# Three stage borders of a hybrid decoder layer: own buffers for the first output-projection weights, first MLP weights split ahead of the norm, operand differences ahead of weight sums

## What is computed

```python
h = modulate(rms_norm(x), shift1, scale1)
y = hybrid_mixer(h, ...)            # ends in concatenate([o_gla, o_hgrn]) @ w_out
x = x + gate1 * y
h = modulate(rms_norm(x), shift2, scale2)
y = square(relu(h @ w_mlp1)) @ w_mlp2
x = x + gate2 * y
return rms_norm(x, final_norm_g)
```

## Time and profile before

| | |
|---|---|
| median of 3 runs | 1274.1 us (1270.65 to 1276.03) |
| the profiled execution | 1274.15 us, its span 1272.4 us |
| TensorE matmul busy | 1174.3 us (92%) |
| VectorE, ScalarE, GpSimd busy | 845.0, 581.1, 484.4 us |
| mean granted TensorE clock | 0.961 |

### The profile page before, as it was taken

One profiled execution on the slowest core, in us unless ns is written; L12 is line 12 of the kernel. 1 busy time (PEld: TensorE's weight loads), 2 busy tenths in 40 slices (PEclk: granted clock), 3 DMA queues, 4 the chain that ended last, 5 costly groups with the idle time before them and its releaser, 6 DMA issues.

```text
span 1272.4 us, 15360 instructions
## 1 busy us (share of the span) xinstructions
PE 1174.3 (92%) x5519; PEld 959.0 (75%) x5519; DVE 845.0 (66%) x970; ACT 581.1 (46%) x865; POOL 484.4 (38%) x286
## 2 busy tenths in 40 slices
PE   4288999989999999699799999999989999999987
PEld 3166778778888887588587888888868888888875
DVE  7978377645454445545498777656796596886965
ACT  4324345444646536324455554554562343424314
POOL 3742101102112112322454434432465575675740
PEclk8589989989999999799999999999989999999999
DMA  8644234101111010434135535345622745547203
GB/s 297 189 155 153 83 117 150 34 17 36 48 33 45 21 50 18 133 97 135 67 99 165 182 133 163 118 158 174 209 72 59 255 128 173 205 125 276 73 1 132
DMA packets 148667, 151.95 MB, mean 119 GB/s; under 512 B 6180, under 2 KB 117880, under 8 KB 145912
## 3 DMA queue, kind: packets, MB, share of 16 engines
q1 hardware_dynamic: 148600, 151.07, 37.0%
HBM read 116.97 MB, written 34.08 MB: 119 GB/s over the span
## 4 chain that ended last, share of the span: by engine, by line
PE 74%; DVE 14%; issue 5%; ACT 4%; POOL 1%; DMA 1%; DVEq 0%; SPq 0%; ACTq 0%; POOLq 0%
PE unit_bank L1221 24%; PE unit_bank L1496 7%; PE unit_bank L1498 7%; PE unit_bank L1497 7%; PE small_bank L1496 7%; PE small_bank L1498 7%; PE small_bank L1497 7%; DVE ada_acc L1549 3%; PE small_bank L1221 2%; PE small_bank L1255 2%; PE small_bank L1344 2%; DVE state L1689 1%; PE small_bank L1336 1%; DVE a_lo L1535 1%; DVE op_lo L1821 1%
## 5 line engine op out<-in xcount | busy, mean ns | idle before, releaser
L1221 PE MATMUL unit_bank<-a_hi,w_hi 128*128 128x512 f32 x592 | 241.9, 409 | 29.9 <-DVE w_lo L1742 12.4
L756 POOL TENSOR_TENSOR wr_lo<-quarter,wr_hi 128x512 fp32r<-128x512 f32 x122 | 197.2, 1630 | 181.1 <-ACT wr_hi L1073 181.1
L1221 PE MATMUL unit_bank<-a_hi,w_lo 128*128 128x512 f32 x592 | 234.7, 397 | 0.0
L1221 PE MATMUL unit_bank<-a_lo,w_hi 128*128 128x512 f32 x592 | 234.5, 396 | 0.0
L693 POOL TENSOR_TENSOR w_lo<-raw,w_hi 128x1024 fp32r<-128x1024 f32 x29 | 75.3, 2595 | 353.2 <-ACT w_hi L795 353.2
L1496 PE MATMUL unit_bank<-op_hi,wr_hi 128*128 128x512 f32 x452 | 179.4, 397 | 18.2 <-POOL wr_lo L756 6.8
L1498 PE MATMUL unit_bank<-op_hi,wr_lo 128*128 128x512 f32 x452 | 178.3, 394 | 0.0
L1497 PE MATMUL unit_bank<-op_lo,wr_hi 128*128 128x512 f32 x452 | 178.0, 394 | 0.0
L1496 PE MATMUL small_bank<-op_hi,wr_hi 128*128 128x512 f32 x452 | 176.6, 391 | 0.0
L1497 PE MATMUL small_bank<-op_lo,wr_hi 128*128 128x512 f32 x452 | 176.0, 389 | 0.0
L1498 PE MATMUL small_bank<-op_hi,wr_lo 128*128 128x512 f32 x452 | 175.9, 389 | 0.0
(11 more groups left out here) (224 smaller groups left out, 1823.8 us busy)
## 6 DMA issues: line engine op xcount, KB each, us to landing
quarter<-in_w_mlp_dram SPq DMA_DIRECT2D x128, 256.0 KB, 4.5
hidden_scratch<-hid SPq DMA_DIRECT2D x98, 256.0 KB, 2.9
ada_slot<-in_w_ada_dram SPq DMA_DIRECT2D x48, 512.0 KB, 4.7
op_full<-hidden_scratch SPq DMA_DIRECT2D x21, 1024.0 KB, 4.8
raw<-in_w_in_dram SPq DMA_DIRECT2D x29, 512.0 KB, 3.7
raw<-in_w_out_dram SPq DMA_DIRECT2D x16, 512.0 KB, 3.9
x_stage<-in_x_dram SPq DMA_DIRECT2D x8, 512.0 KB, 4.1
x_scratch<-xT SPq DMA_DIRECT2D x2, 2048.0 KB, 8.0
```

Source lines behind the costliest of these rows:

```text
L756: pool.tensor_tensor(wr_lo[slot][:, :, :], split_source(n), wr_hi[slot][:, :, :].bitcast(F32), ALU.subtract).then_inc(wr_lo_pool, 1)
L1221: return pe.matmul(out_ap, left, right, start=start, stop=stop)
```

## The change

At border 1, four new buffers `first_w_hi0/1` and `first_w_lo0/1` lie over `k_end`, `k_rel`, `q_rel` and `q_cum`, and hold the weights of output units 0 and 1. ScalarE rounds them after the first quarter of the last gate, VectorE makes the remainders of 0 there, of 1 and 2 behind `low_mixed(0)`, of 3 ahead of `low_mixed(1)`. Units 2 and 3 use the old buffers.

At border 2, `high_weights` 0 and 1 move into the v loop (v = 13), 2 to 6 ahead of `inverse_rms(1)`. The inverse root is a Sqrt on ScalarE and a `reciprocal` on VectorE that writes into the PSUM bank the sum came from; `scale_half` reads that bank. Products 6 and 14, which reuse those banks, wait for the scaling.

At border 3, the P5 parts move one step ahead (DOWN - 2), with both P5 differences; the P6 differences (`second_sum`) stand in step DOWN - 1, and the weight sums and the weight rounding for product 120 move to the end of that step.

```diff
-    parts = {DOWN - 8: (P1,), DOWN - 1: (P5, P3), DOWN: (P2, P7), DOWN + 1: (P6,), DOWN + 2: (P4,)}.get(n, ())
+    parts = {DOWN - 8: (P1,), DOWN - 2: (P5,), DOWN - 1: (P3,), DOWN: (P2, P7), DOWN + 1: (P6,), DOWN + 2: (P4,)}.get(n, ())
...
+        first_w_hi = [at(f"first_w_hi{v}", kb, [P, KT, P], F32R) for v, kb in enumerate((128, 136))]
+        first_w_lo = [at(f"first_w_lo{v}", kb, [P, KT, P], F32R) for v, kb in enumerate((132, 140))]
...
                 if v < 2:
-                    act.wait_ge(unit_filled[1], U_OUT + v - 1)
+                    act.wait_ge(filled["sc" if v else "k"], before("sc" if v else "k", 7))
+                elif v < 4:
+                    act.wait_ge(unit_filled[1], U_OUT + v - 3)
...
+                        if idx == 0:
+                            high_out(0)
+                            high_out(1)
...
                         if half == 1:
-                            high_out(j)
+                            high_out(2 + j)
...
-                act.activation(tok(t0, half), SB[2 + half][:, :], ACT.Ln, bias=eps, scale=1.0 / D
+                act.activation(tok(t0, half), SB[2 + half][:, :], ACT.Sqrt, bias=eps, scale=1.0 / D
                                ).then_inc(read["stat"], 1)
-                act.wait_ge(read["stat"], half + 1)
-                act.activation(tok(t0, half), tok(t0, half), ACT.Exp, scale=-0.5).then_inc(rms_ready, 1)
...
+                if v == 13:
+                    for n in range(2):
+                        high_weights(n)
...
-            for n in range(2):
+            for n in range(2, RING):
                 high_weights(n)
             inverse_rms(1)
-            for n in range(2, RING):
-                high_weights(n)
...
-                if n + RING < PRODUCTS:
+                if n + RING < PRODUCTS and n != DOWN - 1:
                     high_weights(n + RING)
...
                 first_down(n)
+                if n == DOWN - 1:
+                    high_weights(n + RING)
...
                         if idx == 2:
                             low_mixed(0)
+                            low_out(1)
+                            low_out(2)
                         read_out(4 + idx)
                         gate(u0 + 2 + j, 6 + idx, 6 + j, half, idx % 2)
+                        if idx == 0:
+                            low_out(0)
+                    low_out(3)
                     low_mixed(1)
...
+            def inverse_rms(half):
+
+                dve.wait_ge(read["stat"], half + 1)
+                dve.reciprocal(SB[2 + half][:, :], tok(t0, half)).then_inc(rms_ready, 1)
+                dve.wait_ge(rms_ready, 3 + half)
...
-                if n >= 2:
+                if n >= 2 and n != DOWN - 1:
                     hidden_sums(n - 2)
+                if n == DOWN - 2:
+                    hidden_sums(n - 1)
+                if n == DOWN - 1:
+                    for x in range(2):
+                        second_sum(g, x)
                 first_down(n)
+                if n == DOWN - 1:
+                    weight_sums(n + RING)
```

More of the change, by code:

```diff
@@ L436, in out_done, with out_weights @@
             return U_OUT + v % KT + 1
+        def out_weights(v):
+            return (first_w_hi[v], first_w_lo[v]) if v < 2 else (w_hi[(U_OUT + v) % 2], w_lo[(U_OUT + v) % 2])
         def wait_low(e, n):
@@ L1038, in high_half @@
                                ).then_inc(h_high, 1)
[L1040 to L1054, removed]
-            ahead(46, ACT.Ln)
             def high_weights(n):
@@ L1073, in high_weights @@
                 act.activation(wr_hi[slot][:, :, :], split_source(n), ACT.Copy).then_inc(wr_hi_ready, 1)
+            ahead(45, ACT.Sqrt)
+            act.wait_ge(read["ada"], 12)
+            for v in range(OUT_HALVES):
+                half, m = divmod(v, KT)
+                act.wait_ge(unit_read[half], out_done(v))
+                if v >= 4:
+                    act.wait_ge(sum2, v - 2)
+                act.activation(squares[:, v % 4, :], tok(xT[:, m], half), ACT.Square).then_inc(squares2, 1)
+                if 2 <= v < OUT_HALVES - 2:
+                    high_out(v + 2)
+                if v == 9:
+                    inverse_rms(0)
+                if 10 <= v < 14:
+                    for k in range(2 * (v - 10), 2 * (v - 9)):
+                        high_half(0, k)
+                if v == 13:
+                    for n in range(2):
+                        high_weights(n)
             def high_operand(i, src=None):
@@ L1632, in _, with low_out @@
             next_ada = [20]
+            def low_out(v):
+                hi, lo = out_weights(v)
+                dve.wait_ge(whi_ready, U_OUT + v + 1)
+                if v < 2:
+                    dve.wait_ge(filled["o" if v else "sc"], before("o" if v else "sc", 7))
+                elif v < 4:
+                    dve.wait_ge(unit_filled[1], U_OUT + v - 3)
+                dve.tensor_tensor(lo[:, :, :], raw[(U_OUT + v) % 2][:, :, :], hi[:, :, :].bitcast(F32), ALU.subtract
+                                  ).then_inc(wlo_out, 1)
             def group(name, gi, h):
@@ L1735, in group @@
                             low_mixed(0)
+                            low_out(1)
+                            low_out(2)
                         read_out(4 + idx)
                         gate(u0 + 2 + j, 6 + idx, 6 + j, half, idx % 2)
+                        if idx == 0:
+                            low_out(0)
+                    low_out(3)
                     low_mixed(1)
-                    for v in range(2):
-                        slot = (U_OUT + v) % 2
-                        dve.wait_ge(whi_ready, U_OUT + v + 1)
-                        dve.tensor_tensor(w_lo[slot][:, :, :], raw[slot][:, :, :], w_hi[slot][:, :, :].bitcast(F32),
-                                          ALU.subtract).then_inc(wlo_out, 1)
                     return
@@ L1831, in _ @@
                                          ).then_inc(unit_read[half], 1)
-                if v + 2 < OUT_HALVES:
+                if 2 <= v < OUT_HALVES - 2:
                     low_out(v + 2)
                 if v == 10:
-                    dve.wait_ge(rms_ready, 3)
+                    inverse_rms(0)
                     dve.wait_ge(unit_read[0], U_MLP)
@@ L1900, in first_operands @@
                 if n == 2:
-                    dve.wait_ge(rms_ready, 4)
+                    inverse_rms(1)
                     dve.wait_ge(unit_read[1], U_MLP)
```

26 lines of the change are left out of this document (12 added, 14 removed).

## The result

| | before | after |
|---|---|---|
| median | 1272.5 us (1270.7 to 1276.0, 4 runs) | 1252.1 us (1249.3 to 1254.0, 4 runs) |
| profiled execution, span | 1274.15 us, 1272.4 us | 1253.97 us, 1252.2 us |

The account below looks back on a forecast made before the run. TensorE, with matmuls in flight for 92% of the span, was taken as the bound, so only its waits and slow clock could be won. 1274.15 - 14.4 - 7.4 + 1.0 = 1253.3 us, range 1248 to 1259 us.

Parts of the forecast that it names:

- Border 1: Mixer end to output unit 0: minus 14.4 us, from the 12.4 us wait and 2.0 us of slow clock.
- The tightest point: Output unit 4, at 529.1 us: its remainder is ready at 527.8, holding by 1.3 us; otherwise up to 2 us lost.
- Border 2: Output stage into the up projection: minus 7.4 us, 5.35 by product 2 plus 2.06 for the wait at product 20.
- the reciprocal: VectorE's new 512-element operation in the inverse root: 2.7 us, bounds 0.74 and 4.5, from rows of one and eight elements.
- The tail: Behind product 2: the 2.06 us wait at product 20 goes, because VectorE's chain there has slack.
- The second half's norm: VectorE's 5 scalings and 8 remainders end between 634 and 643 us; product 9 needs the last at 642.5, so covered.
- rival 3: Second half's norm late: VectorE's 13 operations all take 1.78 us, product 9 waits about 4 us; 1257 us, chance 0.1.
- Border 3: Products 116 to 118, down projection: plus 1.0 us (minus 1.5 to plus 3); the wait moves to 118, slow clock behind.
- rival 1: Products 116 to 118: the permuted list runs some 6 us faster and 118 does not wait; 1244.7 us, chance 0.1.
- rival 2: Output stage into up projection: the reciprocal takes 4.5 us, so the gain there is 5.6; total 1255.1 us, chance 0.2.
- rival 4: Output units after the mixer: unit 4 or the ordered ScalarE list is late, 3 us handed back; 1256 us, chance 0.1.
- rival 5: Slower than before: the reciprocal costs over 14 us in two chains TensorE follows; at 18 us about 1282 us, chance 0.02.

Follow-up runs that it names:

- the added reciprocal: The changed kernel with one more 128x512 VectorE reciprocal behind the second norm half's own: 312.3 us from product 0 to 114, against 312.0.

## Why the prediction was right

**Border 1** (minus 14.4): 14.65 measured, from unit 0 to unit 10 in both traces, net of the 1.48 us of the earlier stages; alone it gave 14.1. Both terms were right, the wait (12.80 to 0.23 us) and 2.1 us of clock. The tightest point, unit 4, held by 1.1 us where 1.3 were worked out: its remainder runs from 527.75 to 529.53, and the unit begins at 508.83 + 21.76 = 530.59. The last remainder of `low_mixed(0)` ends at 508.3, only half a microsecond ahead of unit 0, but unit 0 waits for them tile by tile and comes to the last one at 513.6: it isn't tight.

**Border 2** (minus 7.4): 7.06 measured (934.25 to 914.02 at product 114, less the 13.17 at unit 10). The terms, net of the earlier parts: product 0 at minus 0.6 (forecast 1.2), product 2 at minus 4.2 (5.35; it starts at 609.38), and 2.86 behind it (2.06, the wait at product 20, which is gone). Two steps were mis-sized. The first is the reciprocal, 3.35 us where two short rows gave 2.7: (3354 - 160) / 511 = 6.25 ns for each further element, not 4.9. By the slope that its doubling showed, one for one, these 0.65 us are what product 0 came later than worked out. The second is the stretch from the end of product 0 to product 2: the forecast took 4.63 us less 0.5 for slow clock, but the clock was back at 2.4 GHz from 619.7 us on, before the sums, and the same stretch takes 4.48 us in after. With product 0 itself (2.87 us, not 2.72) that is the other 0.5 us at product 2. The tail gave 0.8 us more than its term, so the sum came out 0.3 us off: 2.34 around product 20 (the wait and 0.28 us beside it), and 0.5 at products 2 and 9, which ran 0.14 and 0.36 us longer before. That the errors cancel is luck. The forecast's upper bound for the border is also 0.4 us too high: with a reciprocal of 0.74 us its own slope gives 7.4 + 1.96 = 9.4, not 9.8. The waits before units 13 to 15 were forecast at about 1 us each and were 1.57, 0.69 and 0.67; before product 0 it was 1.26 (1.5), with no slow matmuls. From the repeat count of 8 that the Trainium skill ("VectorE: DVE Perf Modes", "First, the fixed hardware budget") gives for the reciprocal, the prediction estimated 4.4 us; the row of 3.35 lies between that estimate and the forecast and decides.

**The second half's norm** (covered): it was, with 4.1 us to spare in after, where the prediction's bounds (634 to 643 against 642.5) gave from none to 8; the added reciprocal showed that it isn't tight. VectorE's sixteen operations ran from 610.93 to 626.34. The scaling with an operand in the bank took 0.73 us in the midst of GpSimd's work, which was the argument against rival 3. The Trainium skill ("SBUF — State Buffer", "Who interferes with whom") says that a VectorE instruction contends with a GpSimd one that reads SBUF when it has two inputs in SBUF, and not when it has at most one; the rows of the kernel with both operands in SBUF agree (1.77 us). But rival 3's price was too high: with four of the eight scalings slow there was no wait. The rule held and the sum beneath it did not matter, for in this stretch GpSimd works only part of the time.

**Border 3** (plus 1.0): plus 1.0 in the two profiled executions (25.03 to 26.03), and the places are nearly as forecast: 0.55 us at product 116, where none was forecast, 6.59 at 118 (7.4), the clock at 0.50 behind it (932.5 to 936.6). In the eleven executions that can be compared the mean is plus 0.1. The anchors say which term was mis-sized. From product 114 to 118 it takes 19.5 to 20.1 us without the edit (mean 19.7) and 17.9 to 18.5 with it (mean 17.9): P2's remainders come 1.8 us earlier, where the forecast had 118 earlier by 1.2. From 118 to 120 it takes 5.6 us without and 7.0 to 8.1 with it (mean 7.4), so the slow clock costs 1.9 us and not 2.2. The gain and the price cancel. The reading that the order of the sums doesn't matter and the length of the list does is what the reordered kernel shows: with four weight sums, the two copies of P1 and a pair of remainders put behind P2's, the whole 6.6 us and the slow clock are gone.

**The rest**: the span fell by 20.20 us = 14.65 + 7.06 - 1.00 + 0.97 (behind product 120: the wait of 2.08 us near the end is followed by seven slow matmuls in the execution of before and by none in that of after, 1.6 us, less 0.6 us of short waits that only after has) - 1.48 (before unit 0). The last two belong to no edit. Rivals 1, 2, 4 and 5 did not come: 118 waits, the reciprocal is under 4.5 us, unit 4 holds. Between the medians of a few runs, differences under 5 us are not worth an argument; the agreement of 20.9 and 20.4 to half a microsecond is partly luck (the same kernel run again came 25.3 us under the kernel before beside it), that of the anchors is not.

## What to carry to other kernels

Where an engine's list between two points is full, its total length sets when the consumer goes on; permuting it moves the wait, and only work put behind the last thing that is needed takes it away. So before reordering, add up what stands ahead of the late item, and ask what of it isn't needed yet. A long stall cost its slow clock too (every one of 4.9 us or more here), and when single edits are worth less than the spread of the early stages, compare distances between anchors of one trace and not whole times.

## What the runs showed that was not expected

- A reciprocal of 128x512 takes 3.34 to 3.36 us whether it writes the bank or SBUF, 6.25 ns for each element past the first, against 0.68 to 0.74 us for other operations of that size with GpSimd idle. The rows of 1 and 8 elements had given 4.9.
- From 500 to 1230 us, waits of 4.9 to 12.4 us of TensorE were followed by 6 to 13 matmuls at 1.2 GHz in every execution. Those of 1.9 us before product 2 were followed by seven or eight in two of three executions; one of 2.06 us before product 20 and all shorter ones were followed by none. At the old border 3 there were 13, 6, 12 and 7 of them in four executions, behind waits of 5.1 to 5.7 us. A wait of 2.08 us near the end of every execution had seven or eight slow matmuls behind it in six of thirteen and none in the others.
- The clock can fall in one execution and not in another behind the same waits: from 150 to 180 us it was granted at 0.89 in one and 1.00 in another, with the same instructions and waits of 1.6 and 1.8 us in both. At the mixer's end the executions of the table are spread over 7.7 us. It is as much as the smaller of the borders gives. What decides it was not tested.
